# Hybrid encoder block on one core: the split products traverse their moving operands and PSUM destinations from the last column to the first

## The reference, cut to what matters

```
h   = rms_norm(x, norm1_g)
z   = h @ w_in                                  # 1024 -> 2056 columns
...                                             # pooling and attention, 8 heads
x   = x + concat([y_pool, y_attn]) @ w_out      # 1024 -> 1024
h   = rms_norm(x, norm2_g)
q   = (h @ w_query)                             # 1024 -> 2048
s1, s2 = q against 2 x 128 sub-keys; top 16 of each, top 16 of the 256 sums, softmax -> gates
for each of the 8 x 16 chosen experts of a frame:
    a = gelu(expert_u[e] . h);  y += gate * a * expert_v[e]
x   = x + y
```

## Time and profile before

| | us |
|---|---|
| median of the runs | 1440.93 |
| fastest run | 1440.38 |
| the profiled execution | 1441.41 |
| its span, first to last instruction | 1439.4 |

### The profile page before, as it was taken

How to read it: one execution, slowest core, us unless ns; L and a number is a source line. 1 busy time by engine, 2 the same in 40 slices (tenths; PEclk the granted TensorE clock), 3 DMA queues, 4 the chain that set the end, 5 groups by cost and what they waited for, 6 DMA issues and landing times.

```text
span 1439.4 us, 20447 instructions
## 1 busy us (share of the span) xinstructions
PE 1431.6 (99%) x7551; PEld 1277.2 (89%) x7551; DVE 1133.4 (79%) x1876; ACT 574.4 (40%) x799; POOL 979.8 (68%) x533
## 2 busy tenths in 40 slices
PE   9999999999999999999999999999999999999998
PEld 7766798899999999999999999888888888888887
DVE  6678551769999999699999995498777777777775
ACT  5775453333333333444444444333333333333332
POOL 3421544346888788866766675599887888878883
PEclk9999999999999999999999999999999999999999
DMA  6221332235778888989999986998888888888883
GB/s 227 103 89 45 103 113 100 89 100 184 251 262 268 273 272 273 348 281 364 355 360 355 372 296 230 371 383 340 346 346 346 327 326 345 344 341 328 331 302 117
DMA packets 122293, 381.57 MB, mean 265 GB/s; under 512 B 11768, under 2 KB 28280, under 8 KB 122240
## 3 DMA queue, kind: packets, MB, share of 16 engines
q1 hardware_dynamic: 70384, 202.69, 39.5%
q0 software_dynamic: 36864, 134.23, 25.3%
q10 hardware_dynamic: 14992, 44.06, 7.8%
HBM read 336.89 MB, written 44.06 MB: 265 GB/s over the span
## 4 chain that ended last, share of the span: by engine, by line
PE 95%; DVE 2%; DMA 1%; ACT 1%; issue 0%; SPq 0%; DVEq 0%
PE bank L748 28%; PE bank L749 28%; PE bank L750 28%; PE bank L1004 6%; PE bank L936 1%; DMA wf<-a_dram 1%; PE bank L884 1%; PE bank L907 0%; PE wide L896 0%; DVE pad L1235 0%; PE bank L815 0%; PE wide L815 0%; PE bank L826 0%; PE bank L822 0%; PE wide L822 0%
## 5 line engine op out<-in xcount | busy, mean ns | idle before, releaser
L484 POOL TENSOR_TENSOR wl<-raw,wh 128x1024 fp32r<-128x1024 f32 x208 | 507.7, 2442 | 277.7 <-ACT wh L514 275.1
L748 PE MATMUL bank<-hh,wh 128*128 128x384 f32 (+1 forms) x1184 | 416.2, 352 | 0.2 <-DVE hl L1251 0.2
L749 PE MATMUL bank<-hl,wh 128*128 128x384 f32 (+1 forms) x1184 | 406.4, 343 | 0.0
L750 PE MATMUL bank<-hh,wl 128*128 128x384 f32 (+1 forms) x1184 | 406.4, 343 | 0.0
L748 PE MATMUL bank<-wh,Wh 128*128 128x512 f32 x768 | 299.0, 389 | 0.7 <-DVE Wl L1458 0.7
L750 PE MATMUL bank<-wh,Wl 128*128 128x512 f32 x768 | 298.8, 389 | 0.0
L749 PE MATMUL bank<-wl,Wh 128*128 128x512 f32 x768 | 298.8, 389 | 0.0
L514 ACT ACTIVATE wh<-raw 128x1024 fp32r<-128x1024 f32 (+1 forms) x217 | 227.8, 1050 | 141.4 <-PE bank L750 136.4
L748 PEld LDWEIGHTS bank<-hh,wh 128*128 128x128 f32 x1184 | 222.8, 188 | 7.9 <-DVE hl L1251 0.6
L749 PEld LDWEIGHTS bank<-hl,wh 128*128 128x128 f32 x1184 | 222.8, 188 | 7.1 <-issue 0.2
L750 PEld LDWEIGHTS bank<-hh,wl 128*128 128x128 f32 x1184 | 222.3, 188 | 7.6
(11 more groups left out here) (200 smaller groups left out, 1628.6 us busy)
## 6 DMA issues: line engine op xcount, KB each, us to landing
raw<-uT_dram SPq DMA_DIRECT2D x128, 512.0 KB
xraw<-v_dram SPq DMA_DIRECT2D x72, 512.0 KB, 8.5
raw<-v_dram SPq DMA_DIRECT2D x56, 512.0 KB, 9.1
a_dram<-act_a ACTq DMA_DIRECT2D x64, 384.0 KB
wf<-a_dram SPq DMA_DIRECT2D x32, 768.0 KB, 6.8
raw<-wst_dram SPq DMA_DIRECT2D x40, 512.0 KB
gates_dram<-gbuf ACTq DMA_DIRECT2D x32, 512.0 KB
gt<-gates_dram SPq DMA_DIRECT2D x32, 512.0 KB, 4.0
```

Source lines behind the costliest of these rows:

```text
L484: pool.tensor_tensor(wl[:, n % SPLIT, :], raw_of(n), wh[:, n % SPLIT, :].bitcast(F32), ALU.subtract).then_inc(w_lo, 1)
L748: pe.matmul(dst, ah, bh, start=start, stop=False)
L749: pe.matmul(dst, ah, bl, start=False, stop=False)
L750: return pe.matmul(dst, al, bh, start=False, stop=stop)
```

## The change

One line at the head of `three` replaces the destination and both moving operands by views of the same columns in reverse order. Column j of the moving operand still meets column j of the destination, so the values are those of before. The stationary operands are not touched, and neither is any wait, buffer, queue or the order or number of the instructions on any engine.

More of the change, by code:

```diff
@@ L746, in three @@
             def three(dst, ah, al, bh, bl, start, stop):
+                dst, bh, bl = (a[:, ::-1] for a in (dst, bh, bl))
                 pe.matmul(dst, ah, bh, start=start, stop=False)
```

## The result

The kernel after takes 1473.39 us (median), the kernel before 1440.8 us beside it. The ratio is 1.023 with a 95% interval of 1.021 to 1.025: 32.6 us slower, just beyond the 2% that count as no change. One of the kernel before's four executions took 8263.65 us and the other three 1440.4 to 1440.9; the ratio goes by the fast ones. The forecast of 1441.0 us, no change, is missed by 32 us; the range to 1760 us holds the result.

The account below looks back on a forecast made before the run. TensorE, busy 1431.6 of 1439.4 us, was taken as the bound. Column, fixed part and other engines were each put at 0; 1439.4 us of span plus the time around it gave 1441.0 us, range 1437 to 1760 us.

Parts of the forecast that it names:

- The bound and the absence of cover: TensorE, busy 1431.6 of 1439.4 us, bounds the kernel; any extra matmul cost in `three` adds to the span in full.
- the rival of the column that pays twice: Descending SBUF read or PSUM write, either enough, doubles each column's time in `three`: 1167 us more, 2608 us; chance 0.17.
- The column. I take 0: Price per column of TensorE's products in `three`: 0 forecast because aligned pairs stay pairs; bounds 0 to 1167 us loss.
- The fixed part. I take 0: The 13.2 ns of each TensorE matmul besides its columns: no change forecast; bounds -82 to +82 us.
- the sign of a wrong picture: Sums for 384 and 512 columns other than their columns allow would refute the split into column price and fixed part.
- both rivals: TensorE's columns at double time, 1167 us, chance 0.17; or each matmul's fixed part doubled, 82 us, chance 0.10.
- The chance of 0.65: Probability given to no change in the whole kernel's time, within 2%, 1412 to 1470 us.
- two rivals that did not occur: On TensorE: fixed part of each matmul doubles, 82 us, chance 0.10; part of the columns pays, 292 us, chance 0.06.
- The other engines: Engines besides TensorE read and write the same tiles in the same order; no term, 0 us.

Follow-up runs that it names:

- e2: Kernel before with only the destination of the split products written from last column to first, moving operands forward: 1440.89 us, ratio 1.0001.
- e3: Kernel before with moving operands and destination backward inside each pair of columns, forward from pair to pair: 1440.31 us, ratio 0.9998.
- e4: Kernel before with moving operands and destination forward inside each pair of columns, backward from pair to pair: 1474.88 us, ratio 1.0232.
- e1: Kernel before with only the two moving operands read from last column to first, destination forward: 1474.12 us, ratio 1.023.
- e9: Kernel before with product groups taking turns: forward, mirrored in blocks of 4, 8, 16 or 64 columns, wholly reversed: 1497.42 us beside 1440.65.
- e7: Kernel before with each split product cut into two of half the columns, all forward: 1633.57 us.
- e10: Kernel before with the weight load reading one stationary column 128 times, moving operands and destination forward: 1459.3 us beside 1440.65.
- e11: Kernel after (moving operands and destination reversed) with the weight load reading one stationary column 128 times: 1465.96 us beside 1440.65.
- e5: Kernel before with moving operands and destination in blocks of 32 columns, blocks descending, forward inside: 1463.71 us beside 1440.55.
- e6: Kernel before with moving operands and destination in blocks of 32 columns, blocks ascending, backward inside: 1479.56 us beside 1440.55.
- e8: Kernel before with each split product cut into two halves, moving operands and destination reversed inside each half: 1624.06 us.

## Why the prediction was right and where it was wrong

**The bound and the absence of cover: right.** The forecast of no change was wrong. What held was its first step, that "whatever a matmul of `three` costs more is added to the span in full", on 3072 products of 384 and 3168 of 512 columns. Times the measured extras they give 34.8 us for a span longer by 31.9, and nearly all of the rest has its place in the mixers and in one wait.

**The destination: right in its value, wrong as a rival.** "Either is enough", said the rival of the column that pays twice. e2 shows that the downward write costs nothing, so half of that rival's case was empty. The rule in the Trainium skill, page "SBUF — State Buffer", section "Door 1: The DMA port swizzle", that a PSUM pattern which is not contiguous slows matmuls much, does not extend to a descending run (e2, 1440.89 us), nor to columns swapped in pairs (e3, 1440.31 us).

**"The column. I take 0": failed, and this with the next step is where the 32 us lie.** Its reason was that columns 511 and 510 are still one pair. That is true, and e3 shows that the order inside a pair is free; but it does not make a descending run free. e4 keeps every pair forward, takes the pairs in descending order and costs all of the loss (1474.88 us, as e1's 1474.12), so going from pair to pair has an order too. The 16-byte line of the same section says full rate as long as neighbours share a line; the prediction read it as "a descending run costs nothing", and that went beyond it. The trace agrees with such a line only at 512 columns, where e9's groups mirrored in 16 bytes keep 226.7 ns; at 384 columns they take 180.8 ns against 174.7 forward.

**"The fixed part. I take 0": the split fails for reversed reads.** The prediction split the pitch into 0.416 ns a column and 13.2 ns. For forward products that is confirmed: it gives 119.8 ns for 256 columns, and e7 measures 120.0. It then offered a loss for either: 82 us for one, 1167 us or a share of it for the other. Measured is a change that belongs to neither, -1.7, +4.45 and +6.66 ns for 256, 384 and 512 columns; the term put at 0 was worth 34.8 us. The two forms show different sums than their columns allow, which the prediction named as the sign of a wrong picture. Because both rivals' prices were derived from that split, no case stood between 5 and 82 us. The chance of 0.65 went to a band that ended at 1470 us. That the range holds 1473 us is luck: it reached to 1760 us for the sake of two rivals that did not occur.

**The full price of the rival "a column pays twice": not seen in any run.** The worst of all patterns tried, mirrored in 16 columns, has 262 to 267 ns for 512 columns, not 440.

**The other engines: right that they set nothing.** No wait of PE appeared that was not there before. ScalarE's wait for the products' last line went from 318.2 to 330.2 us and GpSimd's for ScalarE from 317.9 to 381.4 us, while GpSimd's busy time fell from 979.8 to 948.8 us:

```profile
POOL wl L484 <- ACT wh L514: 381.4, 161, 9.9
ACT wh L514 <- PE bank L751: 330.2, 119, 3.1
```

**What stays open.** e10 and e11 show that the pitch depends on the addresses of the weight load as well as on those of the moving read, and the repeating rows of pitches in e5, e6 and e8 look like two periodic readers that meet. That is an argument only: no view shows where they would meet. Why 16 columns are the worst block, why 4 columns cost at 384 and not at 512, and why 256 columns are better reversed, is not explained. In the patterns by blocks (e5, e6, e9) the destination had the same pattern as the moving operand, and e2 clears only its full reversal; so their prices are those of both together. A reversed weight load was not tried, nor other starting addresses of the tiles. e5 to e11 are single runs.

## What to carry to other kernels

The two directions of a matmul's free axis are not always equal. In this kernel, whose 32-bit operands go at 0.416 ns a column with a weight load beside each matmul, downward reads of the moving operand cost 2.6% of a product of 384 columns and 2.9% of one of 512, and the destination's direction costs nothing. It is no law by size, as 256 columns gained 1.7 ns and another weight load (e11) left 0.6 and 1.7 ns of the loss. So if columns must be mirrored, mirror the destination and not the moving operand (e2 against e1: the same mirrored result, 0 against 32 us). On a kernel in which TensorE is busy for 99% of the span, a difference of 4 to 7 ns in a matmul's pitch is 2% of the time; it shows in the count of matmuls in a fixed stretch (1823 for 1877), from which it can be reckoned without the overlap that the durations hold.

## What the runs showed of the hardware that was not expected

- A matmul's pitch depends on what the weight load beside it reads: 226.67 ns for 512 columns with the ordinary load, 231.67 ns when that load reads one column 128 times (e10).
- Order inside a pair of columns is free (e3). With moving operand and destination mirrored in blocks together, 512 columns cost nothing more in blocks of 16 bytes, up to 5 ns in 32 bytes, 35 to 40 ns in 64 bytes, 10 ns in 128 bytes (e6) and 7 to 13 ns in 256 bytes (e9); 384 columns cost 6 ns more in blocks of 16 bytes, 4 in 32 and 23 in 64, against forward groups in the same run (e9).
- With 256 columns a reversed read was faster than a forward one, 118.2 against 119.9 ns (e8, e7), so a form in which the reversed read gains was there (one run each); it was of no use here, as smaller matmuls lose far more to their number: 1624 us.
- In the stream of equal matmuls with a disturbed read the pitches repeat in short cycles (116, 118, 117, 122 or 123 ns in e8), again and again in the last stage.
